# Moving the block boundary in a two-layer MoE decoder step to the front of the last expert round

## The chip, the cores and the metric

The kernel runs on one core of one Trainium2 chip. The metric is the device time of one execution in microseconds (us): lower is better. TensorE (PE) multiplies matrices into PSUM, VectorE (DVE) and ScalarE (ACT) work on rows, GpSimd (POOL) gathers and does odd jobs, SyncE (SP) does no arithmetic here and issues nearly all DMA transfers.

## The reference

One inference step of a two-layer trunk on 256 prompt tokens and 8 samples (264 columns, held transposed as 8 chunks of 128 features):

```python
for i in range(DEPTH):                      # DEPTH = 2
    mod = silu(c) @ ada_w[i] + ada_b[i]     # shifts, scales, gates: six groups of 1024
    h = modulate(x, norm_mix_g[i], sh1, sc1)
    m = retention_mixer(h, ...) if i % 2 == 0 else gla_mixer(h, ...)
    x = x + g1 * m
    h = modulate(x, norm_ffn_g[i], sh2, sc2)
    f = moe_ffn(h, ...)                     # 64 experts, 8 per token, and a shared one
    x = x + g2 * f
return rmsnorm(x, final_norm_g), new states
```

## The kernel before, in words

The program is a row of blocks: `retention`, `experts(k, 0)`, `gla`, `experts(k, 1)`, `final`. Each block (`with nc.Block()`) holds one instruction list per engine, and ends with a barrier of all five engines, SP among them. `experts` has two blocks: the main one, and a second one (line 3059) for the overflow, in which tokens are worked off that did not fit the slots of their expert. Every engine reads the number of pairs of overflow experts there (`pairs`) and branches over the body when it is 0, as it is with these inputs.

Weights come in 1 MB loads into a ring of 12 slots. `load_until` and `load_round` are SP's lists: for each load SP waits until the load 12 places earlier has been used (`ring_free`), then issues the transfer. TensorE adds to `ring_free` with its last matmul on a slot.

The main block works the 64 experts off in 16 rounds of four (`pe_round`, `round_` of VectorE and of ScalarE). Rounds 14 and 15 are light: each expert has 32 slots, and the whole round is one tile. A round on TensorE: gate products (line 2337), the spread of the round before (line 2395; VectorE adds each of 8 chunks to `acc`, `add_spread`, line 2803), up products, transposes, gathering for the next round, down products (line 2347). In round 15 (`LAST`) SP issues the down weights as eight half loads (line 2252), VectorE adds `acc` to `x` (`add_last`, 8 chunks of three instructions, lines 2806 to 2811), and `last_spread` (line 2380) spreads the round's own rows, which are added to `x` chunk by chunk. Behind these follows, in layer 0, the norm ahead of `gla` (`nxt`, squares at line 505, sums at 524, `Norm.vector`, `Norm.scalar` at 511 and 516) and `cond_products` (line 457); in layer 1 the transposes and sums of squares of the output (`x_rows`, `final_squares`).

Before, SP ends its list of the main block with six loads for the next stage (four of `ada_w`, two of `gla_w_in`), a wait for the remaining slots, and the branch at line 2259. Then come the main block's barrier, the overflow block with its five branches (TensorE's at line 3098) and its barrier, and the block of `gla`, in which SP first issues the two small loads `a1` and `a2` (lines 1316 and 1317), then the rest of the ring. TensorE begins with `project(0, ...)` (line 1361), which reads all 8 chunks of `hT` twice, and then multiplies by `a1` (line 1469).

Of the kernel before, what the change touches and what calls it, by code (L numbers as in the profile page):

```python
# [21 lines left out]
P = 128  # L22
D = 1024
# [106 lines left out]
def build(nc, inp, out):  # L130
    ctx = ExitStack()
    with ctx:
# [3 lines left out]
        def sb(name, cols, dt=F32, parts=P):  # L136
# [7 lines left out]
                    ["ret_state_stored"] + [f"ret_sample_state_stored{b}" for b in range(8)]  # L144
                    + ["gla_state_stored"] + [f"gla_sample_state_stored{b}" for b in range(4)]}
# [46 lines left out]
        experts(k, 0)  # L192
        gla(k)
        sums = experts(k, 1)
        final(k, sums)


# [293 lines left out]
class Norm:  # L491


    def __init__(self, k, layer, which, sq, tmp, root, bank, summed=False):
        self.k, self.layer, self.which = k, layer, which
        self.summed, self.sums_at = summed, k.ps[:, bank, 0:T]
        self.sq, self.tmp, self.root = sq, tmp, root
        self.s_ms, self.s_rt, self.s_prod, self.s_step = (k.sem(f"norm{layer}{which}_{n}") for n in (
            "meansq", "root", "scaled", "vector_step"))
        other = ("chunk", "samples") if summed else ("squared", "summed")  # L500
        self.s_h, self.s_samples = self.s_sq, self.s_sum = tuple(k.sem(f"norm{layer}{which}_{n}") for n in other)
# [5 lines left out]
    def scalar(self, act, next_table=None, turn=0):  # L507

        k, nc = self.k, self.k.nc
        act.wait_ge(self.s_ms, turn + 1)  # L510
# [3 lines left out]
        for c in range(DC):  # L514
            act.wait_ge(self.s_prod, DC * turn + c + 1)
            ins = nc.scalar.activation(k.h[:, c, 0:TP], k.h[:, c, 0:TP], ACT.Identity,
                                       bias=k.mod[:, self.layer, 3 * self.which, c, 0:1])
            if self.summed:
                ins.then_inc(self.s_h, 1)

    def sum(self, pe, c, turn=0):

        pe.wait_ge(self.s_sq, DC * turn + c + 1)
# [4 lines left out]
    def vector(self, v, turn=0):  # L528
# [3 lines left out]
        steps = [3 * turn]  # L532
# [6 lines left out]
        if not self.summed:  # L539
            v.wait_ge(self.s_sum, turn + 1)  # L540
        nc.vector.tensor_scalar(self.tmp, self.sums_at, 1.0 / D, EPS, ALU.mult, ALU.add).then_inc(self.s_ms, 1)
        v.wait_ge(self.s_rt, turn + 1)
# [5 lines left out]
        ins = nc.vector.tensor_tensor(hs, hs, k.mod[:, layer, 3 * which, :, 1:NCOND], ALU.add)  # L548
        if self.summed:
            ins.then_inc(self.s_samples, 1)  # L550
# [45 lines left out]
def retention(k):  # L596
# [60 lines left out]
    s_ldb = [k.stored[f"ret_sample_state_stored{b}"] for b in range(8)]  # L657
    c_out = k.stored["ret_state_stored"]
# [572 lines left out]
def gla(k):  # L1231
# [72 lines left out]
    s_stb = [k.stored[f"gla_sample_state_stored{i}"] for i in range(4)]  # L1304
    c_out = k.stored["gla_state_stored"]
# [7 lines left out]
    with nc.Block() as block:  # L1313
        @block.sync
        def _(sp):
            sp.dma_start(a1, inp["gla_w_a1"][0].rearrange("(c p) r -> p c r", p=P)).then_inc(s_w, 16)
# [7 lines left out]
        def _(pool):  # L1324
            clear_semaphores(pool, old)
            def free(i):
                pool.wait_ge(s_stb[i], 16)
# [3 lines left out]
            def store_prompt(h):  # L1331
                pool.wait_ge(c_s2, h + 1)
                if h:
                    pool.wait_ge(c_out, 16 * h)
# [19 lines left out]
            pool.wait_ge(c_out, 16 * GH)  # L1354

        @block.tensor
        def _(pe):
            def project(t, m, bank, chunks=range(DC)):
# [101 lines left out]
            for t in range(first_gate):  # L1460
# [3 lines left out]
                project(t, 0, 2 * (t % 2))  # L1464
# [7 lines left out]
                elif t == 1:  # L1472
                    pe.wait_ge(s_lowc, 1)
                    for h in range(GH):
                        if h >= 2:
                            pe.wait_ge(s_zc, h - 1)
                        nc.tensor.matmul(k.ps[:, 6 + h % 2, 0:T], a2[:, h * P:(h + 1) * P], low, start=True,
                                         stop=True).then_inc(s_z, 1)
                    cond_transpose(k, k.ps[:, 4], next_rows(k)).then_inc(s_crt, 1)
# [87 lines left out]
        def _(v):  # L1567
            link = lambda ins: k.dve.link(v, ins)
# [46 lines left out]
            def prompt_states(h):  # L1615
                v.wait_ge(s_st, h + 1)
                if h >= 2:
                    v.wait_ge(s_o, h - 1)
                    v.wait_ge(c_out, 16 * (h - 1))
# [147 lines left out]
        def _(act):  # L1767
            def outers(u):
# [156 lines left out]
def final_small(k, pe, small):  # L1925

    for c in range(DC):
        k.nc.tensor.matmul(k.ps[0:NS, 0, 0:1], small[:, c, :], k.ones[:, 0:1], start=(c == 0), stop=(c == DC - 1))


def final(k, sums):
# [5 lines left out]
    meansq, root, rstd = (k.scratch[:, (TT + 1) * D + 4 * i:(TT + 1) * D + 4 * i + TT] for i in range(3))  # L1937
    n_gain = k.stage["final_gain"]
    gain = slot(k, n_gain, D)[:, 0, :]

    with nc.Block() as block:  # L1941
        @block.scalar
        def _(act):
            act.wait_ge(s_ms, 1)
# [8 lines left out]
        def _(v):  # L1953
            nc.vector.scalar_tensor_tensor(meansq[:, 0:2], sums[:, 0:2], EPS, sums[:, 2:4], ALU.add, ALU.add)
# [14 lines left out]
        def _(pool):  # L1969
            wait_slot(k, pool, n_gain)  # L1970
            pool.wait_ge(s_scaled, 1)  # L1971
            nc.gpsimd.tensor_tensor(y[0:NS, 2, :], scaled[0:NS, :], gain[0:NS, :], ALU.mult).then_inc(s_small, 1)

        @block.sync
        def _(sp):
            for t in range(2):
# [9 lines left out]
def experts(k, layer):  # L1986
# [145 lines left out]
    number = extra[0:1, 0:1]  # L2132

# [91 lines left out]
    with nc.Block() as block:  # L2225
        @block.sync
        def _(sp):
# [26 lines left out]
            k.issued = n_end  # L2254
            load_until(k, sp, n_end + KEPT)
            for i in range(KEPT):
                sp.wait_ge(k.ring_free[(n_end + KEPT + i) % RING], (n_end + KEPT + i) // RING)
            sp.wait_ge(s_count, 2)
            with sp.If(sp.value_load(number, min_val=0, max_val=XPAIRS) > 0):
                load_extra(sp, X_LOADS, pair_experts(sp, 0))  # L2260

        @block.gpsimd
        def _(pool):
# [11 lines left out]
            for r in range(LAST + 1):  # L2275
# [5 lines left out]
                if r == 3:  # L2281
                    pool.wait_ge(s_hidtc, PAIRS * 2)
                    pool.wait_ge(s_hid, PAIRS * 2)
                    clear_semaphores(pool, routed)

# [81 lines left out]
        def last_spread(pe, behind):  # L2367
# [891 lines left out]
```

## Time and profile before

| | us |
|---|---|
| three runs | 1614.11, 1618.62, 1620.0 |
| their median | 1618.62 |
| the profiled execution's own time | 1614.77 |
| its span, first to last instruction | 1613.0 |
| TensorE busy | 1516.2 (94%) |
| VectorE, ScalarE, GpSimd busy | 709.3, 364.3, 94.0 |
| mean DMA rate | 360 GB/s, 580.21 MB |

TensorE has work in 94% of the span, and in the expert rounds the DMA engines are full as well. The mean hides the few places where TensorE stands: the change is made at two of these, once in each layer. Engine names with a q behind them are the engine's sequencer, which also executes waits, branches and the parts of a barrier (DRAIN, EVENT_SEMAPHORE).

### The profile page before, as it was taken

To read this page: it belongs to the slowest core of one execution; us is meant where nothing else is said; L and a number is where in the kernel's file an instruction comes from. 1 tells how busy PE (TensorE), PEld (TensorE's weight loads), DVE (VectorE), ACT (ScalarE), POOL (GpSimd) and SP (SyncE) were. 2 spreads that over 40 slices of the span, in tenths; PEclk is the share of its full clock that TensorE was granted. 3 is DMA by queue.
4 is the path that set the end of the run, shared out by engine and by line. 5 is a ranking of instruction groups with operands and counts; after the bars stand their busy time and mean duration, and the time that the engine had idled before them with its cause. 6 is when DMAs were issued, how large, how long until landed. Compare 5 with 4: busy or idle time off the path is not lost. (4 is left out here: it accounts for less than half of the span.)

```text
span 1613.0 us, 29632 instructions
## 1 busy us (share of the span) xinstructions
PE 1516.2 (94%) x11206; PEld 1009.5 (63%) x11206; DVE 709.3 (44%) x1980; ACT 364.3 (23%) x770; POOL 94.0 (6%) x119
## 2 busy tenths in 40 slices
PE   6999999998999999999997799999999999999986
PEld 4778765776665665565554487767566556565553
DVE  3205535215465355345454235443745534543453
ACT  3002443103111121112111244431111111211112
POOL 0000110001000000000000000001000000010000
PEclk9999999999999999999999899999999999999998
DMA  9997799339999999999999793988999999999896
GB/s 364 388 370 266 259 394 404 124 98 367 393 420 420 420 421 420 419 420 419 398 370 409 265 291 110 351 305 325 420 420 421 421 420 420 420 419 410 338 420 248
DMA packets 153578, 580.21 MB, mean 360 GB/s; under 512 B 17181, under 2 KB 62401, under 8 KB 105226
## 3 DMA queue, kind: packets, MB, share of 16 engines
q1 hardware_dynamic: 137642, 535.74, 83.8%
q0 software_dynamic: 15200, 40.92, 6.6%
q10 hardware_dynamic: 640, 2.26, 0.4%
q8 instruction: 61, 1.00, 0.3%
q14 instruction: 35, 0.29, 0.0%
HBM read 567.17 MB, written 26.90 MB: 368 GB/s over the span
## 5 line engine op out<-in xcount | busy, mean ns | idle before, releaser
L2431 PE MATMUL ps<-ring,scratch 128*64 128x256 f32 x3328 | 367.8, 380 | 10.0 <-DMA ring<-in_moe_w_up 8.8
L2431 PEld LDWEIGHTS ps<-ring,scratch 128*64 128x64 f32 x3328 | 245.0, 137 | 121.6 <-issue 14.3
L2497 PE MATMUL ps<-ring,scratch 128*64 128x512 f32 x896 | 200.5, 598 | 0.0
L698 PE MATMUL ps<-hT,ring 128*128 128x264 f32 x768 | 182.5, 392 | 1.3 <-ACT hT L380 1.3
L2836 DVE SCALAR_TENSOR_TENSOR scratch<-scratch,ps 128x256 f32<-128x256 f32 x62 | 29.8, 481 | 327.4 <-ACT scratch L2985 313.4
L2395 PE MATMUL ps<-scratch 128*128 128x264 bf16 x1392 | 169.6, 276 | 1.5 <-DVE scratch L2803 1.5
L698 PEld LDWEIGHTS ps<-hT,ring 128*128 128x128 f32 x768 | 147.6, 194 | 31.4 <-issue 2.8
L2395 PEld LDWEIGHTS ps<-scratch 128*128 128x128 bf16 x1392 | 121.8, 97 | 50.2 <-issue 14.3
L2803 DVE TENSOR_TENSOR scratch<-scratch,ps 128x264 f32<-128x264 f32 x240 | 102.6, 430 | 86.3 <-PE ps L2395 86.0
L2497 PEld LDWEIGHTS ps<-ring,scratch 128*64 128x64 f32 x896 | 58.1, 136 | 117.7 <-issue 86.2
L2985 ACT ACTIVATE scratch<-ps 128x256 f32<-128x256 f32 x62 | 23.8, 384 | 424.6 <-PE ps L2431 356.3
L2164 POOL DMA_INDIRECT scratch<-h_rows,scratch x60 | 59.8, 997 | 897.9 <-DVE scratch L2158 889.3
L3015 ACT CAST scratch<-ps 128x512 bf16<-128x512 f32 x116 | 68.0, 586 | 145.2 <-PE ps L2497 139.9
L1361 PE MATMUL ps<-hT,ring 128*128 128x264 f32 x384 | 91.9, 396 | 9.5 <-PEq L3059 9.5
L2897 DVE TENSOR_TENSOR scratch<-ps,scratch 128x512 f32<-128x512 f32 x116 | 79.7, 687 | 25.9 <-ACT scratch L3015 25.9
L1361 PEld LDWEIGHTS ps<-hT,ring 128*128 128x128 f32 x384 | 74.1, 196 | 23.4 <-issue 10.3
L2887 DVE TENSOR_TENSOR scratch<-scratch 128x512 bf16<-128x512 f32 x116 | 80.4, 693 | 4.0
L2311 PE MATMUL ps<-tab,scratch 128*128 128x128 f32 x480 | 65.1, 279 | 13.0 <-DVE scratch L2631 9.7
L2311 PEld LDWEIGHTS ps<-tab,scratch 128*128 128x128 f32 x480 | 51.8, 141 | 24.7 <-DVE scratch L2631 16.4
L955 DVE SCALAR_TENSOR_TENSOR ring<-ring,rstd 128x512 f32<-128x512 f32 x64 | 41.3, 687 | 49.7 <-ACT rstd L1108 36.7
L2631 DVE COPY scratch<-ps 128x512 f32<-128x512 f32 x60 | 41.5, 692 | 48.5 <-PE ps L2311 48.5
L859 PE MATMUL ps<-scratch,ring 128*128 128x264 f32 x256 | 57.7, 387 | 0.0
(402 smaller groups left out, 1458.3 us busy)
## 6 DMA issues: line engine op xcount, KB each, us to landing
ring<-in_moe_w_gate SPq DMA_DIRECT2D x128, 1024.0 KB, 20.1
ring<-in_moe_w_up SPq DMA_DIRECT2D x128, 1024.0 KB, 21.9
ring<-in_moe_w_down SPq DMA_DIRECT2D x120, 1024.0 KB, 18.0
ring<-in_ada_w SPq DMA_DIRECT2D x48, 1024.0 KB, 12.4
ring<-in_ret_w_in SPq DMA_DIRECT2D x24, 1024.0 KB, 16.7
ring<-in_state_ret SPq DMA_DIRECT2D x16, 1024.0 KB, 14.0
out_ret_sample<-ring POOLq DMA_DIRECT2D x16, 1024.0 KB, 9.2
ring<-in_gla_w_in SPq DMA_DIRECT2D x12, 1024.0 KB, 12.0
```

The source lines that it names most:

```text
L698: mm = nc.tensor.matmul(k.ps[:, bank, 0:T], w[:, c, m * P:(m + 1) * P], k.h[:, c, :], start=(c == 0), stop=(c == DC - 1))
L859: mm = nc.tensor.matmul(k.ps[:, out_bank(n), 0:T], w[:, c, m * P:(m + 1) * P], vo[:, 4 * h + c, :], start=(h == 0 and c == 0), stop=(h == ...
L1361: mm = nc.tensor.matmul(k.ps[:, bank, 0:T], w[:, c, m * P:(m + 1) * P], k.h[:, c, :], start=(c == 0), stop=(c == DC - 1))
L2164: pool.indirect_dma_start(xtok_of(p), None, h_rows[:, :], bass.IndirectOffsetOnAxis(ap=rows[:, p:p + 1], axis=0), bounds_check=ABSENT - 1, ...
L2311: mm = nc.tensor.transpose(k.ps[:, b, c * P:(c + 1) * P], xtok_of(p)[:, d0:d0 + P], ident)
L2395: mm = nc.tensor.matmul(k.ps[:, c % 2, 0:T], parts_of(p)[:, s, c * P:(c + 1) * P], slot_token[:, p, :], start=(p == 0 and s == 0), stop=(p ...
L2431: mm = nc.tensor.matmul(k.ps[lo:lo + CAP, 2 + p, j * DE:(j + 1) * DE], xg[:, p, c, lo:lo + CAP], slot(k, n, DE)[:, c, :], start=(c == 0), ...
L2497: mm = nc.tensor.matmul(k.ps[lo:lo + CAP, 6 + half, :], hid_t[:, p, m, lo:lo + CAP], slot(k, n, D)[:, m, half * 512:(half + 1) * 512], sta ...
L2803: nc.vector.tensor_tensor(acc[:, c, :], acc[:, c, :], k.ps[:, c % 2, 0:T], ALU.add).then_inc(s_add, 1)
L2887: nc.vector.tensor_tensor(parts_of(p)[:, 2, cols], rest[:, half], parts_of(p)[:, 1, cols], ALU.subtract).then_inc(s_part, 1)
L2897: nc.vector.tensor_tensor(rest[:, half], k.ps[:, 6 + half, :], parts_of(p)[:, 0, cols], ALU.subtract).then_inc(s_rest, 1)
L3015: nc.scalar.copy(parts_of(p)[:, 0, cols], k.ps[:, 6 + half, :]).then_inc(s_rhi, 1)
```

## The change

The main block of `experts` now ends after round 14. All that follows is returned as an object `tail` with one function per engine, which `gla` (or `final`) calls at the top of its own block: the last round, the overflow path, the norm behind it (in layer 1 the output's sums). The overflow block is gone. Each engine reads the number of pairs at the end of the main block (`read_pairs`, a wait, a register load and a check) and takes one branch at the top of the next block: with pairs, round 15 and the overflow; without (`Else`), round 15 and the following sums. SP's loads of round 15 stay in the main block. Its loads of the next stage come behind the barrier: twelve without a wait for an overflow, then a wait for the norm's sums (`behind.norm.s_sum`), then `a1` and `a2`. `gla`'s first projection waits for `hT` chunk by chunk. In round 14 VectorE adds `acc` to `x` ahead of `hidden`, and in round 15 adds the spread of round 14 straight to `x` (three instructions a chunk in place of one). ScalarE runs a dummy square root in both layers behind the branch. Clearing of semaphores moves to the end of `gla`'s GpSimd list, and one set of store semaphores serves both mixers.

```diff
 experts: SP, end of main block
-            k.issued = n_end
-            load_until(k, sp, n_end + KEPT)
-            for i in range(KEPT):
-                sp.wait_ge(k.ring_free[(n_end + KEPT + i) % RING], (n_end + KEPT + i) // RING)
-            sp.wait_ge(s_count, 2)
-            with sp.If(sp.value_load(number, min_val=0, max_val=XPAIRS) > 0):
-                load_extra(sp, X_LOADS, pair_experts(sp, 0))
+            read_pairs(sp, "sp")
...
 experts: TensorE, end of main block
-            for r in range(HEAVY - 2, LAST + 1):
+            for r in range(HEAVY - 2, LAST):
                 pe_round(pe, r)
-            last_spread(pe, x_rows if layer else nxt.sum)
...
+            read_pairs(pe, "pe")
...
+        def vector_round(v, r, late=0, beside=None):
...
+            if last:
+                for c in range(DC):
+                    v.wait_ge(s_scat, DC * (r - 1) + c + 1)
+                    add_last(v, c, k.ps[:, c % 2, 0:T], DC + c).then_inc(s_add, 1)
+            elif light(r):
+                add_spread(v, r - 1)
+                v.wait_ge(s_add, DC * (r + 1))
+                for c in range(DC):
+                    ins = add_last(v, c, acc[:, c, :], c)
+                k.dve.link(v, ins)
...
+    def tail_sync(sp):
+
+        k.issued = n_end
+        load_until(k, sp, n_end + KEPT)
+        pairs = extra_pairs["sp"]
+        with sp.If(pairs > 0):
...
+        load_until(k, sp, n_end + RING)
...
+    def tail_tensor(pe):
...
+        with pe.If(pairs > 0):
+            pe_round(pe, LAST)
+            last_spread(pe, None)
...
+        with pe.Else():
+            pe_round(pe, LAST)
+            last_spread(pe, follow)
+            for c in range(DC - 2, DC):
+                follow(pe, c)
...
+        nc.scalar.activation(silu[0:1, 0, 0:1], ident[0:1, 0:1], ACT.Sqrt)
...
 gla
         @block.sync
         def _(sp):
+            behind.sync(sp)
+            sp.wait_ge(behind.norm.s_sum, 1)
             sp.dma_start(a1, inp["gla_w_a1"][0].rearrange("(c p) r -> p c r", p=P)).then_inc(s_w, 16)
...
+                    if first:
+                        pe.wait_ge(behind.norm.s_h, c + 1)
```

## Rows read from the trace of the kernel before

**Rows 1.** Windows: stretch, its length, busy us by engine, PEclk, DMA share, GB/s.

```profile
840.00:850.00 10.00, 10.00 (x112) 5.72 (x109) 6.95 (x17) 1.56 (x3) 0.99 (x1) 1.00 1.02 423
...
912.00:914.00 2.00, 2.00 (x6) 1.58 (x5) 0.00 (x0) 0.00 (x0) 0.00 (x0) 0.50 0.67 178
...
916.00:918.00 2.00, 2.00 (x11) 1.71 (x10) 0.00 (x0) 0.00 (x0) 0.00 (x0) 1.00 1.10 348
```

**Rows 2.** Timeline, TensorE in round 15 of layer 0: start, us, what, [idle before].

```profile
866.58 5.89 PE L2337 MATMUL ps<-ring,scratch 128*32 128x256 f32 x64 [5.33 <-DMA ring<-in_moe_w_gate]
872.40 0.85 PE L2395 MATMUL ps<-scratch 128*128 128x264 bf16 x6
...
876.53 3.66 PE L2337 MATMUL ps<-ring,scratch 128*32 128x256 f32 x64
```

**Rows 3.** Timeline of SP's issues around the same round, and its last piece alone.

```profile
861.73 15.41 SPq L2252 DMA_DIRECT2D ring<-in_moe_w_down  x8
877.18 5.12 SPq L300 DMA_DIRECT2D ring<-in_ada_w  x4
882.34 10.51 SPq L300 DMA_DIRECT2D ring<-in_gla_w_in  x2
...
876.08 1.05 SPq L2252 DMA_DIRECT2D ring<-in_moe_w_down  x1
```

**Rows 4.** Sources of two barriers, lines 2225 and 1313: duration in ns, first and last start.

```profile
L2225 SPq DRAIN  x2: 7/7/7, 893.9 to 1598.4; - x2
...
L1313 PEldq DRAIN  x1: 737/737/737, 1067.8 to 1067.8; - x1
L1313 SPq DRAIN  x1: 116/116/116, 1069.2 to 1069.2; - x1
L1313 SPq EVENT_SEMAPHORE  x1: 17/17/17, 1069.5 to 1069.5; - x1
```

**Rows 5.** Source of TensorE's overflow branch, min/median/max ns, layer 0 and layer 1.

```profile
L3098 PEldq COMPARE_BRANCH  x2: 334/2028/3722, 905.4 to 1604.6; - x2
```

**Rows 6.** Timeline, VectorE: adding two chunks of a spread, then chunks added to x.

```profile
873.05 0.77 DVE L2803 TENSOR_TENSOR scratch<-scratch,ps 128x264 f32<-128x264 f32 x2 [9.04 <-PE ps L2395]
...
885.43 0.17 DVE L2806 TENSOR_TENSOR scratch<-ps,mod 128x8 f32<-128x8 f32 x1 [0.24 <-PE ps L2380]
...
885.98 0.16 DVE L2806 TENSOR_TENSOR scratch<-ps,mod 128x8 f32<-128x8 f32 x1
```

**Rows 7.** Timeline from the norm of layer 0 into the next mixer.

```profile
900.52 3.30 ACT L516 ACTIVATE hT<-hT,mod 128x256 f32<-128x256 f32 x8 [3.04 <-DVE hT L552]
...
909.55 10.30 PE L1361 MATMUL ps<-hT,ring 128*128 128x264 f32 x32 [9.46 <-PEq L3059]
...
919.78 3.73 PE L1469 MATMUL ps<-hT,scratch 128*16 128x264 f32 x16
...
923.45 7.39 PE L1361 MATMUL ps<-hT,ring 128*128 128x264 f32 x32
```

**Rows 8.** DMA issues of 855 to 925: KB each, median us from issue to landing.

```profile
ring<-in_ada_w SPq DMA_DIRECT2D x4, 1024.0 KB, 14.4
scratch<-in_gla_w_a SPq DMA_DIRECT2D x1, 64.0 KB, 2.6
```

**Rows 9.** Timeline of layer 1: TensorE in round 15, SP's last two pieces.

```profile
1574.39 5.27 PE L2337 MATMUL ps<-ring,scratch 128*32 128x256 f32 x64 [5.96 <-DMA ring<-in_moe_w_gate]
...
1584.33 3.66 PE L2337 MATMUL ps<-ring,scratch 128*32 128x256 f32 x64 [0.60 <-DMA ring<-in_moe_w_up]
...
1582.38 1.71 SPq L2252 DMA_DIRECT2D ring<-in_moe_w_down  x2
```

**Rows 10.** Timeline of the end: ScalarE's last sum, then the final block.

```profile
1598.99 0.20 ACT L3039 ACTIVATE scratch<-tab 1x1 f32<-1x1 f32 x1
...
1603.29 0.20 ACT L1920 ACTIVATION_READ_ACCUMULATOR scratch<-ps 128x1 f32 x1
1605.35 1.28 ACT L1945 ACT_TABLE_LOAD   x1 [1.86 <-PEq L3059]
...
1606.64 0.20 ACT L1945 ACTIVATE scratch<-scratch 128x3 f32<-128x3 f32 x1
```

More of the change, by code:

```diff
@@ L191, in build @@
         retention(k)
[L192 to L195, printed above, removed]
+        behind = experts(k, 0)
+        gla(k, behind)
+        behind = experts(k, 1)
+        final(k, behind)
 def retire_semaphores(k):
@@ L497, in __init__, with scalar @@
         self.sq, self.tmp, self.root = sq, tmp, root
[L498 to L501, printed above, removed]
+        self.s_ms, self.s_rt, self.s_prod, self.s_step, self.s_h, self.s_samples = (
+            k.sem(f"norm{layer}{which}_{n}") for n in ("meansq", "root", "scaled", "vector_step", "chunk", "samples"))
+        if not summed:
+            self.s_sq, self.s_sum = (k.sem(f"norm{layer}{which}_{n}") for n in ("squared", "summed"))
     def square(self, act, c):
         return self.k.nc.scalar.activation(self.sq[:, c, :], self.k.x[:, c, :], ACT.Square).then_inc(self.s_sq, 1)
-    def scalar(self, act, next_table=None, turn=0):
+    def scalar(self, act, next_table=None):
         k, nc = self.k, self.k.nc
-        act.wait_ge(self.s_ms, turn + 1)
+        act.wait_ge(self.s_ms, 1)
         nc.scalar.activation(self.root, self.tmp, ACT.Sqrt).then_inc(self.s_rt, 1)
@@ L1228, with gla @@
 GLA_OUT_BANK = [0, 1, 2, 4, 5, 6, 3, 7]
-def gla(k):
+def gla(k, behind):
     nc, inp, out = k.nc, k.inp, k.out
@@ L1463, in _ @@
                     pe.wait_ge(s_qk, 2 * (t - 1))
-                project(t, 0, 2 * (t % 2))
+                if t == 0:
+                    pe.wait_ge(behind.norm.s_samples, 1)
+                project(t, 0, 2 * (t % 2), first=t == 0)
                 project(t, 1, 2 * (t % 2) + 1).then_inc(k.ring_free[loads[t] % RING], 1)
@@ L1767, in _ @@
         def _(act):
+            behind.scalar(act)
             def outers(u):
@@ L1927, in final_small, with final @@
     for c in range(DC):
-        k.nc.tensor.matmul(k.ps[0:NS, 0, 0:1], small[:, c, :], k.ones[:, 0:1], start=(c == 0), stop=(c == DC - 1))
-def final(k, sums):
+        mm = k.nc.tensor.matmul(k.ps[0:NS, 0, 0:1], small[:, c, :], k.ones[:, 0:1], start=(c == 0), stop=(c == DC - 1))
+    return mm
+def final(k, behind):
     nc, out = k.nc, k.out
@@ L1943, in _ @@
         def _(act):
+            behind.scalar(act)
             act.wait_ge(s_ms, 1)
@@ L2365, in slots_first, with last_spread @@
             mm.then_inc(s_ht, 1)
-        def last_spread(pe, behind):
+        def last_spread(pe, follow):
             d = done_tiles(LAST, 0)
@@ L2381, in last_spread @@
                                      start=True, stop=True).then_inc(s_scat, 1)
-                    if half:
-                        behind(pe, c - 2)
+                    if half and follow:
+                        follow(pe, c - 2)
         def spread(pe, r, late=0, n=PAIRS):
```

758 lines of the change are left out of this document (380 added, 378 removed).

## The prediction

> **What bounds the kernel now.** I read the windows first. In the expert rounds TensorE is busy for the whole of a window and the DMA engines are full too, at 423 GB/s [rows 1]; a delay handed to TensorE there is not won back later, since neither has slack. Then I went to the two places which the change touches and read the timeline of every engine there, because what counts at a barrier is who arrives last. Three things are to be seen.
>
> First, TensorE stands before round 15 in both layers: the gate products start at 866.58 after 5.33 us of waiting for weights, in layer 1 at 1574.39 [rows 2, 9]. Second, SP is later still: its eight half loads of the down weights take 15.41 us to issue, the last ends at 876.08 + 1.05 = 877.13, and only at 877.18 does it issue the loads whose slots TensorE gave back around 872.4 [rows 2, 3]. SP is held by the transfer queue being full, not by a semaphore. Third, the old boundary comes after all this: ScalarE's last `hT` chunk is done at 900.52 + 3.30 = 903.82, TensorE starts the projections at 909.55, 9.46 us after its last matmul [rows 7].
>
> **The barrier, which moves.** It includes SP: SP has a DRAIN in the main block's barrier at 893.9, 1.05 us behind its last issue (882.34 + 10.51 = 892.85), and in that time it had read `pairs` and branched [rows 3, 4]. In the barrier that closes the `gla` block SP is the last: TensorE has drained at 1067.8 + 0.74 = 1068.5, SP at 1069.2 + 0.12 = 1069.3, and the release is at 1069.5, 0.2 us later [rows 4]. SP's drain does not wait for transfers in flight, only for its own list.
>
> The change leaves SP's eight half loads ahead of the barrier and puts TensorE's round 15 behind it. So round 15, which now waits for the gate weights until 866.58, will wait for SP to have *issued* the last down weights. SP arrives at 877.13 + 1.05 = 878.2, the release is at 878.4. Queued behind it: round 15 on TensorE, VectorE and ScalarE, the norm, the ring's next loads.
>
> **The branch.** TensorE's branch over the overflow body took 3.72 us in layer 0 and 0.33 us in layer 1, the same instruction with the same outcome [rows 5]. The new branch jumps over a body that holds all of round 15 as well, so its target is further away. I take 3.72 us in both layers; 0.33 us is the lower bound. For the upper bound I take two such stalls, 7.44 us, since the new branch runs while the queues are full, and the old ones did not.
>
> The Trainium skill ("Runtime: NRT & Kernel Launch", Instruction fetch mechanics) says that a taken branch with a target outside the fetched window stalls for a fetch, which agrees with the slow row, and that TensorE's instruction memory holds 2048 instructions, more than this body; by that figure the target could be there after the long wait at the barrier, and the sum would be that of the short branch.
>
> **Layer 0, in order.**
> - Round 15 starts at 878.4 + 3.7 + 0.1 = 882.2 in place of 866.58: +15.6 (12.2 with the short branch).
> - Gate products took 5.89 us after a pause of 5.33, and 3.66 for the same 64 at full clock [rows 2]. After the 9.46 us pause the projections still ran at 0.50 until 914 and at 1.00 from 916: 10.30 us against 7.39 [rows 1, 7], so about 2.9 us extra. The new pause is some 20 us. Between 5.89 and twice 3.66 = 7.3 I take 6.5, near 3.66 + 2.9: +0.6.
> - The spread of round 14 now ends in three VectorE instructions a chunk, at a pitch of 0.55 us (885.43 to 885.98), in place of 0.385 (0.77 for two) [rows 6]. TensorE alternates two banks, so each pair of chunks waits once for a VectorE step that is 0.17 longer, four times: about +0.5 with a hand-over.
> - `acc` added to `x` in round 14 instead of round 15: 8 x 0.55 = 4.4 us of VectorE. Removed from round 15 it gains nothing: after it VectorE still waited 0.24 us for TensorE [rows 6]. Added to round 14 it stands ahead of `hidden` and delays that round by some 1.3 us, which is covered: TensorE ended round 14 at 866.58 - 5.33 = 861.25 [rows 2], 17 us before SP arrives. Without that cover it would cost the 1.3 us.
> - Dummy square root: 0.20 us [rows 10], on the path in layer 0. +0.2.
> - So the norm is +16.9. Its `hT` chunks come from 900.94 + 16.9 = 917.8 to 920.7. With the chunk-wise wait and no barrier, the first eight-chunk pass takes 3.7 us (half of 7.39) from 917.9 and ends at 921.6, the second at 925.3. The clock should be full, the pause being under 1 us. Before, this point was 919.78 [rows 7]: +5.5. The change thus saves 11.4 us here, 5.7 of barrier and branch, 2.8 of overlap, 2.9 of clock, and gives 16.9 for it.
> - `a1` now stands behind twelve ring loads in SP's queue. The first four can start when the gates are done, 882.2 + 6.5 = 888.7; at 2.7 us each (386 GB/s) and eight at 3.0 us (1.05 MB at 348 GB/s [rows 1]) the stream ends at 923.5, and `a1` needs 2.6 us from issue to landing on an empty queue [rows 8], so 924 to 926. TensorE wants it at 925.3. I put +0.5, with 0 and 3 as ends.
> Sum of layer 0: +6.0.
>
> The Trainium skill ("DMA: Bandwidth & Descriptors", Queues, rings and completion order) says that completion is not in order per issuing engine, by which `a1` might land ahead of the last ring loads; the term would then be 0.
>
> Semaphore clearing moves behind GpSimd's last wait of `gla`, where the block's end is set by SP and TensorE [rows 4]; nothing, and what it would cost without that cover are some register-sized instructions on GpSimd. Store semaphores shared: nothing. The rounds and `gla` between are bound by TensorE, so the shift is carried whole.
>
> **Layer 1.** SP's last piece ends at 1582.38 + 1.71 = 1584.09 [rows 9]; + 1.05 + 0.2 + 3.7 + 0.1 = 1589.2 against 1574.39: +14.8. Gates 6.5 for 5.27: +1.2. Spread +0.5, less the 0.60 that the up products waited for weights [rows 9]. Together +15.9 to ScalarE's last sum. Gained behind it: from 1603.49 to the square root at 1606.64 lie two barriers and a table load of 1.28 us [rows 10]; in one list, behind a square root already run, what remains is three small VectorE instructions, about 0.55 us: -2.6. Sum: +13.3.
>
> **Total.** 6.0 + 13.3 = +19.3. On the profiled execution: 1614.8 + 19.3 = 1634.1. The median of the runs is 3.9 above it, which would give 1637.9; the lowest run is 0.7 below it. I give 1636.
>
> **Rivals.**
> - *Short branch.* Both branches cost 0.33: -3.4 in layer 1; in layer 0 about -2.5, as `a1` then lands after TensorE wants it. 1628 on the profile, up to 1632. For it: layer 1's row.
> - *Longer stalls.* Two fetches behind full queues, or `a1` 3 us late: +8 to +11, 1642 to 1648.
> - *SP does not hold the barrier.* If it has issued its last load by the time the gates land (866.6), round 15 starts when it did. Then TensorE wants `a1` at about 908.5, but the twelve loads cannot end before some 921 (the round's own four up and eight half down loads end at 866.6 + 8 x 2.48 = 886.4 at 423 GB/s, then 34.8 for the twelve), so layer 0 is still +2 to +3 and layer 1 -2.6 + 0.5: no change, 1615. Against it: the rows of SP.
> - *Faster.* As before, and `a1` passes the ring loads. Then layer 0 gains 11.4 less 1: the mechanism is the whole old boundary leaving the path, at two places. Layer 0 gains as long as round 15 starts less than 11.4 - 1.3 = 10.1 us late, before 876.7, so with 4.0 for release and branch SP must arrive before 872.7. Full price, with SP there before the gates land: 1614.8 - 10.4 - 2.1 = 1602. Against it: SP arrives at 878.2 in this trace, and issues the same list at the same rate afterwards.
>
> **How the numbers follow.** Forecast 0.60, short branch 0.15, longer stalls 0.12, SP early 0.07, faster 0.06. The measurement can tell about 0.5%, 8 us, from no change. Slower by more: 0.60 + 0.15 + 0.12 = 0.87; within: 0.07; faster: 0.06. Range 1624 to 1648: it takes in the first three cases.
>
> **What would show it.** In the new trace: the main block's barrier with SP draining last, near 878 and 1585; gates of round 15 starting near 882 and 1589 with the barrier as releaser, in place of a DMA; TensorE's branch row, of 0.3 or 3.7 us; the DMA engines empty for a few us before the `ada_w` loads; `project` starting about 1 us behind the norm's first chunk; ScalarE's last square root without a table load. If SP drains before 867, the forecast is wrong at its root; if the gates start below 880 it is the branch that I have mis-sized.

## The result and the profile after

| | before | after |
|---|---|---|
| median of four runs, us | 1617.43 | 1641.47 |
| lowest to highest, us | 1614.11 to 1620.0 | 1640.37 to 1643.62 |
| the profiled execution's own time | 1614.77 | 1642.50 |
| its span | 1613.0 | 1640.7 |

The changed kernel is slower: the ratio is 1.0151, with an interval of 1.0128 to 1.0175. That is +24.0 us between the medians and +27.7 between the two spans. The difference between these is the choice of executions: the profiled one before lies 2.7 below its median, the one after 1.0 above it. What follows compares spans.

The page of after shows where the time is not. TensorE is busy for as long as before (1516.2 then), and nearly the same bytes are moved (580.21 MB then):

```profile
PE 1517.1 (92%) x11206; PEld 1006.4 (61%) x11206; DVE 712.9 (43%) x2012; ACT 363.5 (22%) x770; POOL 94.1 (6%) x119
...
DMA packets 153580, 580.23 MB, mean 354 GB/s; under 512 B 17181, under 2 KB 62401, under 8 KB 105226
```

So the 27.7 us are time in which TensorE stands, waits or runs at its lower clock. TensorE's timeline around round 15 of layer 0, answering to [rows 2], shows most of one half of it:

```profile
858.57 0.50 PE L2434 MATMUL ps<-tab,scratch 128*128 128x128 f32 x2 [1.98 <-DVE scratch L2768]
...
885.59 5.46 PE L2359 MATMUL ps<-ring,scratch 128*32 128x256 f32 x64 [21.94 <-issue]
890.98 0.85 PE L2418 MATMUL ps<-scratch 128*128 128x264 bf16 x6
...
895.83 3.66 PE L2359 MATMUL ps<-ring,scratch 128*32 128x256 f32 x64
```

The gate products of round 15 start at 885.59, after a pause of 21.94 us; before, at 866.58 after 5.33 [rows 2]. The releaser is no DMA any more. Who held TensorE is in two other views: SP's timeline, and the source rows of the barrier, of the branch behind it and of VectorE's branch (duration in ns, start in layer 0 to start in layer 1).

```profile
864.12 13.82 SPq L2279 DMA_DIRECT2D ring<-in_moe_w_down  x8
...
1581.74 14.32 SPq L2279 DMA_DIRECT2D ring<-in_moe_w_down  x8
```

```profile
L2252 PEldq DRAIN  x2: 2032/2124/2215, 861.8 to 1579.5; - x2
L2252 ACTq DRAIN  x2: 14/16/18, 864.6 to 1582.5; - x2
L2252 DVEq DRAIN  x2: 95/96/97, 866.3 to 1584.2; - x2
L2252 SPq DRAIN  x2: 7/7/7, 878.6 to 1596.7; - x2
...
L2252 PEldq EVENT_SEMAPHORE  x2: 51/51/51, 878.8 to 1596.9; - x2
...
L3106 PEldq COMPARE_BRANCH  x2: 6212/6224/6237, 878.9 to 1597.0; - x2
...
L3179 DVEq COMPARE_BRANCH  x2: 63/63/63, 878.9 to 1597.0; - x2
```

Read down the starts of the DRAINs. VectorE is ready at 866.3 and SP at 878.6, so four engines stand for 12 us for one that is still issuing transfers. Its eight half loads end at 864.12 + 13.82 = 877.94, and the release follows 0.2 us behind its drain. The last four of the eight wait for no semaphore (`ring_free` stands ahead of the first four only), and their issues take 1.0 to 4.5 us each, where the quickest of the eight take 0.5: SP is held in issuing itself, while the DMA engines are full. Then TensorE's branch takes 6.2 us, in both layers. The late round also empties the memory system: SP's next loads wait for slots that round 15 gives back, and the first of them is issued at 891.06. The window ahead of it (the last number is the rate in GB/s; the kernel before has 408 in the same window):

```profile
885.00:890.00 5.00, 4.41 (x49) 2.44 (x52) 0.00 (x0) 0.00 (x0) 0.00 (x0) 0.57 0.26 97
```

Further on in layer 0, at the seam to the next mixer (timeline, answering to [rows 7]):

```profile
919.72 3.30 ACT L515 ACTIVATE hT<-hT,mod 128x256 f32<-128x256 f32 x8 [3.05 <-DVE hT L547]
...
920.37 7.36 PE L1364 MATMUL ps<-hT,ring 128*128 128x264 f32 x32 [1.17 <-ACT hT L515]
...
920.40 2.92 SPq L1314 DMA_DIRECT2D scratch<-in_gla_w_a  x1
923.36 2.92 SPq L1315 DMA_DIRECT2D scratch<-in_gla_w_a  x1
...
930.26 5.39 PE L1474 MATMUL ps<-hT,scratch 128*16 128x264 f32 x16 [2.54 <-DMA scratch<-in_gla_w_a]
...
935.59 7.39 PE L1364 MATMUL ps<-hT,ring 128*128 128x264 f32 x32
```

The first projection starts beside the norm, 0.65 us behind its first chunk, where before 9 us lay between [rows 7]: the gain that the change has here is real. But the 16 products with `a1` start 2.54 us after TensorE could have begun them, and take 5.39 us at a lower clock for 3.73. By 935.59 the shift is +12.1.

Which transfer they waited for has to be read from the code as well. `a1` (line 1314) and `a2` (line 1315) raise one semaphore, and TensorE waits ahead of the `a1` products until both have landed (`pe.wait_ge(s_w, 32)`, with 16 for each load), though `a2` is multiplied only one projection later. The view of the DMA issues:

```profile
scratch<-in_gla_w_a SPq DMA_DIRECT2D x1, 64.0 KB, 7.9
scratch<-in_gla_w_a SPq DMA_DIRECT2D x1, 32.0 KB, 6.9
```

`a2` has landed at 923.36 + 6.9 = 930.26, and this is when the products start. `a1` is put at 920.40 + 7.9 = 928.3, 0.6 us behind the end of the projection (920.37 + 7.36 = 927.7); as both raise one semaphore, the split between them is the profile's estimate. So the last to come is `a2`.

Layer 1, round 15 and the end (timeline, answering to [rows 9, 10]):

```profile
1603.59 6.55 PE L2359 MATMUL ps<-ring,scratch 128*32 128x256 f32 x64 [22.02 <-issue]
...
1633.77 0.20 ACT L1929 ACTIVATION_READ_ACCUMULATOR scratch<-ps 128x1 f32 x1
...
1634.39 0.20 ACT L1957 ACTIVATE scratch<-scratch 128x3 f32<-128x3 f32 x1 [0.42 <-DVE scratch L1971]
```

The gates start 29.2 us later than before, of which 11.9 are brought along (the barrier at the end of `gla` is released at 1081.4, before at 1069.5). From ScalarE's last sum to the square root are 0.62 us and no table load, in place of 3.35 with one [rows 10].

### The profile page after: what moved, and what is told of

The parts are those of the page before. It is cut to its first block and busy times, and to the rows that moved or that the text cites. A ratio compares the mean times of both kernels' runs of the same rounds, so it can differ in the third digit from the quotient of the medians.

```text
span 1640.7 us, 29626 instructions
## 1 busy us (share of the span) xinstructions
PE 1517.1 (92%) x11206; PEld 1006.4 (61%) x11206; DVE 712.9 (43%) x2012; ACT 363.5 (22%) x770; POOL 94.1 (6%) x119
## 5 line engine op out<-in xcount | busy, mean ns | idle before, releaser
L2735 DVE TENSOR_TENSOR scratch<-scratch,ps 128x264 f32<-128x264 f32 x224 | 96.4, 431 | 66.3 <-PE ps L2418 66.0
L2359 PE MATMUL ps<-ring,scratch 128*32 128x256 f32 x512 | 34.0, 424 | 44.0 <-issue 44.0
## 6 DMA issues: line engine op xcount, KB each, us to landing
ring<-in_gla_w_in SPq DMA_DIRECT2D x12, 1024.0 KB, 11.5
```

Of the source, the lines that this page charges most:

```text
L2359: mm = nc.tensor.matmul(k.ps[lo:lo + 32, bank, j * DE:(j + 1) * DE], xg_of(p)[:, c, lo:lo + 32], slot(k, n, DE)[:, c, :], start=(c == 0), ...
L2735: nc.vector.tensor_tensor(acc[:, c, :], acc[:, c, :], k.ps[:, c % 2, 0:T], ALU.add).then_inc(s_add, 1)
```

## The experiments

Three causes are in the trace: SP, the branch, and the wait for `a1` and `a2`. The rivals are that they cover each other (whoever takes away one finds the next), or that the round is held by something else behind the barrier: the empty transfer queues, or the three instructions a chunk. Each cause is taken away alone, then all three together, and one part of the change is put into the kernel before by itself. Each kernel's ratio is to the kernel before on its own chip (thirteen runs with a median of 1615.34 for the first four, 29 with 1615.22 for the others). The changed kernel's own ratio rests on only four runs before, so what a kernel takes away from it is given twice, by the medians and by the ratios (times 1616):

| kernel | median | ratio | less than after: by medians | by ratios |
|---|---|---|---|---|
| half loads behind the barrier | 1624.75 | 1.0057 | 16.7 | 15.2 |
| shortened body | 1638.85 | 1.0143 | 2.6 | 1.3 |
| empty body | 1629.47 | 1.0088 | 12.0 | 10.2 |
| early `a1` | 1638.70 | 1.0134 | 2.8 | 2.7 |
| loads, `a1` and empty body | 1608.01 | 0.9960 | 33.5 | 30.9 |
| exchanged bodies | 1635.07 | 1.0128 | 6.4 | 3.7 |
| loads, `a1` and exchanged bodies | 1612.06 | 0.9982 | 29.4 | 27.3 |

**SP's list: the eight half loads go behind the barrier.**

```diff
 experts: SP, main block
-            expert_of = [expert_at(sp, LAST * EPI + e) for e in range(EPI)]
-            for half in range(2):
...
-                    sp.dma_start(slot(k, n, D)[:, :, cols], expert_weight("moe_w_down", expert_of[e])[:, :, cols])\
-                        .then_inc(s_first_half if half == 0 else k.ring_full[n % RING], 16)
             read_pairs(sp, "sp")
...
     def tail_sync(sp):
+        expert_of = [expert_at(sp, LAST * EPI + e) for e in range(EPI)]
+        for half in range(2):
...
```

> The changed kernel with one edit: SP issues round 15's eight down-weight loads behind the barrier, as the first thing in the next block, in place of ahead of it. Theory (the barrier waits for SP's issuing): VectorE now drains last, near 866.3, the release is near 866.5, and with the same 6.2 us branch the gate products of round 15 start near 873.3 in layer 0 (885.6 in the changed kernel) and near 1591 less what layer 0 gains in layer 1 (1603.6). Layer 1 gains about 12. Layer 0 gains only about 4 of its 12, because the small load a1 still stands behind twelve ring loads, whose stream cannot begin before the round's own weights are in. Sum about -15 to -16 against the changed kernel: 1.005 to 1.007 of the kernel before, near 1626. Rival (the barrier is held by something else, such as the transfers in flight): the start stays at 885, ratio 1.015.

Measured: 1624.75 (ten runs), ratio 1.0057 (1.0038 to 1.0075), as expected. Barrier, branch and round of that kernel:

```profile
L2252 SPq DRAIN  x2: 7/7/7, 857.4 to 1568.6; - x2
...
L2252 DVEq DRAIN  x2: 97/99/101, 866.3 to 1575.9; - x2
L3108 PEldq COMPARE_BRANCH  x2: 6189/6200/6212, 866.7 to 1576.3; - x2
...
873.24 6.29 PE L2350 MATMUL ps<-ring,scratch 128*32 128x256 f32 x64 [9.59 <-issue]
...
922.49 5.48 PE L1474 MATMUL ps<-hT,scratch 128*16 128x264 f32 x16 [6.29 <-DMA scratch<-in_gla_w_a]
```

Now SP drains first and VectorE last, at 866.3 as in after, and the gates start 12.35 us earlier, which is the stretch from 866.3 to 878.6. That SP held the barrier is thereby shown, not read off alone. The branch is as long with SP's list out of its way, so its 6.2 us don't hang on the long wait ahead of it (between TensorE's last product and the branch lie 3 us here and 15 there). And the wait for `a1` and `a2` has grown from 2.54 to 6.29 us: TensorE came 11.5 us earlier, the issue of `a2` only 7.8. This is a cause covered by another.

**The branch: the body that is jumped over is shortened.** First, of TensorE's body with pairs, the last round is left out and the overflow kept:

```diff
         with pe.If(pairs > 0):
-            pe_round(pe, LAST)
-            last_spread(pe, None)
...
```

> The changed kernel with one edit: on TensorE the body that is branched over holds the overflow alone, as in the kernel before, without round 15 (left out is thus round 15 in the case of an overflow, which these inputs don't have). Theory (the stall of 6.2 us comes from the length of the jump): it falls to 0.3 to 3.7 us, as in the kernel before, in each layer; -5 to -12 in sum, 1630 to 1636. Rival (it comes from full transfer queues, which the branch of the kernel before did not meet): it stays at 6.2 us in both layers and the time at 1641.

Measured: 1638.85 (four runs), ratio 1.0143 (1.0111 to 1.0175): a miss. The branch is as short as was expected, and the time hardly moved. The rows say why:

```profile
L3106 PEldq COMPARE_BRANCH  x2: 342/354/367, 878.7 to 1595.2; - x2
...
879.43 1.03 PE L2359 MATMUL ps<-ring,scratch 128*32 128x256 f32 x2 [16.06 <-PEq L2252]
885.33 5.16 PE L2359 MATMUL ps<-ring,scratch 128*32 128x256 f32 x62 [4.87 <-issue]
```

The round begins at 879.43, executes two products, and then stands for 4.87 us, with "issue" as its releaser, which means nothing that the profile shows. In layer 1 the same happens with 2.10 us, after 29 products. So the stall is not bound to the branch instruction. My reading is that it is the time until instructions of the new place are there: in layer 0 the first 2 products were at hand, in layer 1 the first 29. Why the same body differs so between the layers, these runs don't say; in both the stall ends 6.4 to 6.6 us behind the start of the branch, much as in the changed kernel (6.2). Whoever reads the branch row alone takes this for a gain of 6 us.

The profile bears the reading out. In its view of the DMA queues one transfer on a queue that it calls "instruction" lies within the 6.2 us of the branch in after (window 878.9 to 885.1 in layer 0):

```profile
q8 instruction: 1, 0.02, 1.1%
```

Narrowed down, it starts at 882.55 and takes 1.05 us (layer 1: 1600.73 and 1.15). In each stall of these traces there is one such transfer, of 16 KB, and TensorE goes on 1.3 to 1.6 us behind its end: both layers of this kernel, of after, of the one with the half loads moved and of the one with early `a1`, layer 0 of the exchanged bodies below, and the slow branch of the kernel before. There it starts 1.0 us behind the branch, in after 3.7, which is about the difference between 3.7 and 6.2 us. Such transfers also occur where nothing stands, so it is the constant distance that speaks, not their presence.

Then the whole body is left out, one wait remains:

```diff
         with pe.If(pairs > 0):
-            pe_round(pe, LAST)
...
-            for c in range(DC):
-                follow(pe, c)
```

> The changed kernel with one edit: on TensorE the body that is branched over holds one wait and nothing else (left out is the overflow's arithmetic, not needed with these inputs). Theory (the stall is a fetch of instructions for a far target): 0.1 to 0.35 us in both layers, gates of round 15 start at 879.5 in place of 885.6; about -6 in each layer, 1629 to 1630, ratio 1.007 to 1.008. Rival (any taken branch behind a barrier costs this): 6.2 us stays.

Measured: 1629.47 (four runs), ratio 1.0088 (1.0057 to 1.0119), as expected.

```profile
L3106 PEldq COMPARE_BRANCH  x2: 213/220/226, 877.9 to 1590.2; - x2
...
878.58 5.07 PE L2359 MATMUL ps<-ring,scratch 128*32 128x256 f32 x64 [15.93 <-PEq L2252]
...
923.34 6.65 PE L1474 MATMUL ps<-hT,scratch 128*16 128x264 f32 x16 [3.02 <-DMA scratch<-in_gla_w_a]
```

All 64 gate products run through from 878.58, with no second stall. The jump thus costs 6.0 us a layer (6.22 less 0.22; a further 1.0 us of the earlier start in layer 0 is SP, which was through at 877.6 in this execution). It is the distance that costs: the comparison, the outcome and the barrier ahead of it are the same.

**`a1`: a copy of it loaded ahead of the ring loads, to a place that is free then.**

```diff
-    a1 = on_flat[:, 0:DC * RANK].rearrange("p (c r) -> p c r", c=DC)
+    a1 = k.rstd[:, 2 * T:2 * T + DC * RANK].rearrange("p (c r) -> p c r", c=DC)
...
         def _(sp):
+            sp.dma_start(a1, inp["gla_w_a1"][0].rearrange("(c p) r -> p c r", p=P)).then_inc(s_w1, 16)
             behind.sync(sp)
...
-                    pe.wait_ge(s_w, 32)
+                    pe.wait_ge(s_w1, 16)
...
+                    pe.wait_ge(s_w, 16)
```

The edit does two things: `a1` comes early, and its products no longer wait for `a2`, which is waited for one projection later (the last line, with the products of `a2`).

> The changed kernel with one edit: the small load a1 goes to a place that is free already and is issued at the start of the next block, ahead of the ring loads, with a semaphore of its own; a2 stays behind. Theory (a1 behind twelve ring loads costs 2.5 us of waiting and 1.7 us of slower products after it): -4.2 us, all in layer 0, 1637, ratio 1.012 to 1.013; the products with a1 take 3.7 us again in place of 5.4 and start without a DMA in front. Rival (TensorE then waits for something else, such as the next ring load): no gain.

Measured: 1638.7 (four runs), ratio 1.0134 (1.0102 to 1.0166), as expected. Its interval overlaps with that of after, so the runs alone don't separate the two; the trace does:

```profile
881.16 0.41 SPq L1313 DMA_DIRECT2D rstd<-in_gla_w_a  x1
...
923.28 7.36 PE L1365 MATMUL ps<-hT,ring 128*128 128x264 f32 x32 [1.17 <-ACT hT L515]
930.57 3.73 PE L1475 MATMUL ps<-hT,rstd 128*16 128x264 f32 x16
934.24 7.39 PE L1365 MATMUL ps<-hT,ring 128*128 128x264 f32 x32
```

From the first projection to the second are 934.24 - 923.28 = 10.96 us, in after 935.59 - 920.37 = 15.22. So the wait for the two costs 4.3 us, 2.5 of standing and 1.7 of clock. How much of it the split of the semaphore alone would have saved was not run. This execution came 2.9 us later to the first projection (round 14 was late already, ahead of the place that the edit touches), which hides it in the time.

**All three together** (half loads behind the barrier, early `a1`, no body to jump over):

> The changed kernel with three edits together: down loads behind the barrier, a1 ahead of the ring loads (behind the down loads), and on TensorE a body to branch over that holds one wait (left out is the overflow's arithmetic on TensorE, not needed with these inputs). Theory (three costs, and nothing else, stand between the change and its gain): round 15 starts when its gate weights are in, near 868, as in the kernel before; layer 0 is 9 to 10 us ahead of the kernel before at the products with a1, layer 1 gains another 1 to 2 at the end. Sum -9 to -12 against the kernel before, ratio 0.993 to 0.995. Rival (the moved work has a cost of its own that the three hide): ratio 0.998 or above.

Measured: 1608.01 (ten runs), ratio 0.996 (0.9948 to 0.9973). This is faster than the kernel before, by 7.2 us between the medians, but less than was expected (9 to 12, 0.993 to 0.995; only the interval reaches into that). Alone, the three took away 31.5 by the medians and 28.1 by the ratios; together they take away 33.5 and 30.9. Within the noise, some 3 us for each ratio, they add up. But a fourth cost has come out from behind them.

```profile
868.01 5.28 PE L2352 MATMUL ps<-ring,scratch 128*32 128x256 f32 x64 [4.45 <-DMA ring<-in_moe_w_gate]
...
903.36 7.36 PE L1365 MATMUL ps<-hT,ring 128*128 128x264 f32 x32 [1.16 <-ACT hT L515]
910.65 3.73 PE L1475 MATMUL ps<-hT,rstd 128*16 128x264 f32 x16
...
924.45 3.15 PE L1484 MATMUL ps<-scratch 16*128 16x264 f32 x8 [2.75 <-DMA scratch<-in_gla_w_a]
```

The gates wait for their weights again, as before the change, and `a1` is multiplied 9.1 us earlier than before it (910.65 to 919.78 [rows 7]). This is what the moved boundary is worth when nothing holds it: the 11.4 us that the prediction's sum has for the barrier, the overlap and the clock, less the 1.4 by which the gates start later and the 0.7 of the longer spread.

Of the 9.1 us most is lost again at the next small load. `a2` was left behind the ring loads, is issued at 914.78 and takes 9.5 us to land, and its products at 924.45 wait 2.75 us for it. Behind the pause the granted clock (the last column but two) is at half:

```profile
926.00:928.00 2.00, 2.00 (x6) 1.07 (x5) 0.00 (x0) 0.93 (x3) 0.00 (x0) 0.50 1.09 346
```

From these products to the same later point of the mixer (975.00, before 978.03) it takes 50.55 us, before 47.26: 3.3 us more. So 2.75 + 3.3 = 6.0 of the 9.1 us are gone; 3.0 are left at that point and 3.3 at the end of `gla`. In layer 1 the gates start 3.9 us earlier than before, the end brings another 2.7, and 6.6 is what the spans differ by (1606.4 to 1613.0). None of the other kernels waits there, since in each the `a2` products come later or an earlier wait has covered `a2`. `a2` loaded early as well was not run; by these rows, as an estimate, it would bring up to 6 us more.

**The same, with the overflow kept: TensorE's two bodies change places.** The last round without overflow stands directly behind the branch, the one with overflow behind it, so that the far jump comes after the round.

```diff
-        with pe.If(pairs > 0):
+        with pe.If(pairs < 1):
+            pe_round(pe, LAST)
+            last_spread(pe, follow)
...
+        with pe.Else():
             pe_round(pe, LAST)
             last_spread(pe, None)
...
```

Alone on the changed kernel:

> The changed kernel with the exchange of TensorE's two bodies alone. Theory: round 15 starts 6 us earlier in both layers, at 879.5 and accordingly; layer 1 keeps the 6, layer 0 gives the stall back between the sums and the projection, but then no longer waits for a1, so it keeps 3 to 4.5. Sum -9 to -11 against the changed kernel, 1631, ratio 1.009 to 1.010. Rival (the jump behind the sums costs nothing): as with the empty body, 1629 or less, ratio 1.008.

Measured: 1635.07 (four runs), ratio 1.0128 (1.0113 to 1.0143): a miss, less of a gain than was expected.

```profile
L3106 PEldq COMPARE_BRANCH  x4: 83/2460/6609, 879.1 to 1622.8; - x4
...
879.61 6.16 PE L2359 MATMUL ps<-ring,scratch 128*32 128x256 f32 x64 [15.62 <-PEq L2252]
...
916.26 6.59 PE L456 MATMUL ps<-ring,condT 128*32 128x256 f32 x64 [5.95 <-issue]
...
933.77 7.39 PE L1364 MATMUL ps<-hT,ring 128*128 128x264 f32 x32
```

The 6.0 us are won at the gates (879.61 for 885.59), and in layer 0 lost again behind the norm's sums: TensorE stands for 5.95 us at the jump to the common code (6609 ns in the branch row is this jump), and the 64 products behind the pause take 6.59 us for 3.66. The windows of this stretch show the granted clock (the last column but two) at half, 1.2 GHz, from the pause on:

```profile
914.00:916.00 2.00, 0.00 (x0) 0.00 (x0) 2.00 (x6) 1.58 (x4) 0.00 (x0) 0.50 1.07 353
...
918.00:920.00 2.00, 2.00 (x24) 0.96 (x20) 0.63 (x2) 0.00 (x0) 0.00 (x0) 0.50 1.14 356
```

The norm of the other engines goes on meanwhile and hides a part; the second projection starts 1.8 us earlier than in after, and no more. In layer 1 this jump comes at 1622.8, behind TensorE's last product, and is over after 4.84 us, while the last stores are still going out, so that nothing waits for it directly. Of the 8.4 us by which the span is shorter, 6.6 come from layer 1. It could have been 8.4 there: the last square root comes 10.2 us earlier (1624.20 for 1634.39), but from it to the end it takes 8.1 us for 6.3, as SP is released later behind its last stores; why, these runs don't say. (By the ratios the gain is only 3.7; the profiled execution is this kernel's fastest, and the ratio of after rests on few runs. How much of the miss is that stays open.)

All three, with the bodies exchanged:

> The same, but with the overflow kept: on TensorE the two bodies are exchanged, so that the one without overflow is fallen into and the jump over the overflow's body stands behind it; in layer 1 nothing follows the jump, in layer 0 the products with the condition and the next mixer do. Theory: layer 1 pays nothing for the jump; layer 0 pays 5 to 6 us between the norm's sums and the first projection, where only about 1 us was free. Sum -3 to -6 against the kernel before, ratio 0.996 to 0.998. Rival (a jump at the end of a straight run is fetched ahead): as the run without a jump, 0.993 to 0.995.

Measured: 1612.06 (twelve runs), ratio 0.9982 (0.9972 to 0.9993), on the side of faster, at the weak edge of what was expected, and by less than the 0.5% that the prediction wanted to call it a change.

```profile
869.50 5.35 PE L2352 MATMUL ps<-ring,scratch 128*32 128x256 f32 x64 [3.82 <-DMA ring<-in_moe_w_gate]
...
906.39 5.85 PE L456 MATMUL ps<-ring,condT 128*32 128x256 f32 x64 [5.94 <-issue]
```

Of the versions that still work off an overflow, this is the fastest. The one without a jump is 4 us faster. The row of `L456` has the jump, 5.94 us and a lower clock behind it; it is more than 4, but TensorE comes late enough for `a2` here and doesn't pay the 6.0 us that the other pays there.

**`acc` into `x` in round 14, alone on the kernel before:**

```diff
+                if last:
+                    for c in range(DC):
+                        v.wait_ge(s_scat, DC * (r - 1) + c + 1)
+                        add_last(c, k.ps[:, c % 2, 0:T], DC + c).then_inc(s_add, 1)
+                elif light(r):
                     add_spread(r - 1)
...
+                        ins = add_last(c, acc[:, c, :], c)
```

> The kernel before with one part of the change alone: the accumulator is added to x in round 14, and round 15 adds the spread of round 14 straight to x. Theory (the part costs little and gains nothing by itself): round 14 on TensorE ends 1.3 us later, covered by the wait for the gate weights at 866.6; the spread in round 15 takes 4.9 us in place of 4.1, in layer 1 hidden behind the up weights. Sum 0 to +1.5 us, ratio 1.000 to 1.001. Rival (the 4.4 us of VectorE taken out of round 15 had been on the path): -4 to -8 us, ratio 0.995 to 0.998.

Measured: 1615.04 (ten runs), ratio 0.9998 (0.9986 to 1.0009). This part moves nothing that can be measured, by itself too: its 1.3 us in round 14 fall into the wait for round 15's gate weights.

## Why the prediction was right, and where its sizes were off

The direction was right, and so was the mechanism at its root: SP's drain came last in the barrier, forecast at 878.2, measured at 878.6; in layer 1, with the shift of 11.9 brought along, 1597.0 was forecast and 1596.7 measured. Undoing that alone took away 15.2 us by the ratios, of 24.4.

The time was forecast as 1636 and measured as 1641.5; on the profiled execution, 1634.1 against 1642.5. So 8.4 us are missing from the sum. Two terms hold them, and a third is small.

- *The branch.* The term was 3.7 us in each layer, the slow one of the two rows of the kernel before [rows 5], and it measured 6.2: 2.5 twice. It lies between my value and the upper bound of two stalls, 7.4. The choice went wrong at a step that I had written down, that the target is further away, and then not priced: I took the row of a short jump for a long one. The empty body shows 0.2, the shortened one 0.35 with 4.9 us one place later. The rule of the Trainium skill ("Runtime: NRT & Kernel Launch", Instruction fetch mechanics) that a taken branch out of the fetched window stalls for a fetch agrees with the long rows and with the instruction transfer inside each stall; it leaves open why the same branch took 0.33 us in layer 1 of the kernel before. That the target might be there after the long wait, which I had worked out from that page's size of the instruction memory, did not come true, neither after 15 us of waiting nor after 3.
- *`a1`.* The term was 0.5 us with 3 as its upper end; it measured 4.2, outside my bounds. What failed first is a wait that the sum left out. I had priced the landing of `a1` alone, and the products wait for `a1` and `a2` on one semaphore. `a2` is issued 2.96 us behind `a1`, as the issue of `a1` itself holds SP for 2.92 us, and needs 6.9 us to land. By the profile's split `a1` was late by 0.6 us, near my 0.5, and the other 1.9 us of standing are `a2`. That the 0.5 fits so well is in part luck, since both sides of it lay later than I had them, TensorE at 927.7 for 925.3 and `a1` at 928.3 for 924 to 926. I had used the 2.6 us of an empty queue [rows 8], and the landings took 7.9 and 6.9.
  Both stood behind megabytes of ring loads that were issued but not through, and I had let the stream end first and then added the latency of an idle queue. The second omission is the clock: even a wait of 2.5 us cost 1.7 more in the products behind it (5.39 for 3.73), which the bound of 3 did not hold. Windows of after, in the pause and behind it:

```profile
928.00:930.00 2.00, 0.00 (x0) 0.00 (x0) 0.00 (x0) 0.42 (x2) 0.00 (x0) 1.00 1.09 331
930.00:932.00 2.00, 1.74 (x5) 0.58 (x5) 0.00 (x0) 0.00 (x0) 0.00 (x0) 0.56 1.08 349
```

  By the rule of the Trainium skill ("DMA: Bandwidth & Descriptors", Queues, rings and completion order) that completion isn't in order the term would have been 0. The trace agrees with the rule in a small way: the ring load issued just ahead at 917.43 took 12.1 us and landed at 929.5, 1.2 us behind where the profile puts `a1`. But that was not enough to make the wait vanish; what brought it to 0 was the issue ahead of the ring loads, with a semaphore of its own.
- *The start of the round and the gates in layer 0.* SP 0.4 later and the first product 0.5 instead of 0.1 behind the branch; against that, the gate products took 5.4 (from 885.59 to 890.98) for 6.5. With the 0.2 of the longer spread this comes to -0.1. In layer 1, 6.5 was forecast and 6.5 measured.

The rest held. The spread: 4.85 us for 4.13, so +0.7 for a forecast of +0.5. The dummy square root and the chunk-wise start of the first projection: shift of +19.2 at the norm's last step and of +7.95 at the end of the first projection, so 11.3 us saved there for a forecast of 11.4. The end of layer 1: -2.7 for -2.6. `acc` in round 14: nothing, and the run by itself says so too; its 1.3 us are in the trace (the transposes of round 14 waited 1.98 us for VectorE, with 0.68 before) and covered. And layer 0's sum, 6.0 + 2.4 (the branch's 2.5 less that 0.1) + 3.7 = 12.1, and layer 1's, 13.3 + 2.5 = 15.8, meet the 11.9 and 15.8 of the spans.

Of the rivals, the short branch and SP's being early are out by the rows. "Longer stalls", 1642 to 1648, came nearest in its mechanism: a longer fetch and a late small load. (Full queues as its reason were not tested by themselves.) The measured time lies 0.5 below its lower end, and I had given it 0.12. The forecast's own 0.60 was too much for a sum whose two soft terms could only be seen at shorter jumps and in an empty queue. The rival that ends on the faster side was not this kernel's case, but its mechanism, the old boundary leaving the path, is what the kernel with all three taken away shows. The rival's full price was 1602, 12.8 below the profiled execution; the runs give 7.2 between the medians. The trace has where the rest went: 6.0 us to the wait for `a2` and the clock behind it. Small parts are gates that start 1.4 us later than before and a wait of 0.35 us for the up weights in layer 0, where before there was none.

Open is how far a jump may go before it costs. Three lengths were run, and what the shortest of them left standing was one wait.

## What to carry to other kernels

Before moving a barrier, write down when each engine arrives at the new place, the one that only issues transfers too: a full transfer queue holds it as surely as a semaphore, and here that was over half of the loss. Price a jump by its distance, and look for its stall at the first instructions behind it, not in the branch row alone; a rare path is best laid so that the common path never jumps over it where somebody waits. A small transfer that is needed early has to be issued ahead of the large ones: behind them it took 7 to 10 us to land where 2.6 sufficed, and the wait cost clock on top. Before pricing a transfer, read the wait in the code: if it counts two transfers, the later one sets it. And after taking a cost away, look in the new trace for the next wait, which the old costs had covered.

## What the runs showed of the hardware

- A taken far jump on TensorE took 6.2 us in both layers, with 15 us of waiting ahead of it or 3. At another place (the exchanged bodies) TensorE stood 5.95 us for it, and at the very end of the kernel its row has 4.84 us. With a shorter one the branch took 0.35 us and the stall came 2 products later (4.87 us) or 29 products later (2.10 us).
- In each of these stalls, except the one at the very end, which no product follows, TensorE went on 1.3 to 1.6 us behind the end of a transfer of 16 KB on the queue named "instruction".
- VectorE stands as well, in layer 0 alone, and its branch row doesn't show it: 63 ns at 878.9, and its first operation of the new block comes at 884.59, 5.7 us behind the branch; in layer 1 at 1597.51, 0.5 us behind it. The other kernels with the moved boundary have 5.4 to 5.8 us in layer 0. That this too is a fetch is likely and not shown. TensorE's own jump hid it, and where that was gone the gate products did: with the empty body VectorE's first operation came at 883.64, as these ended (878.58 + 5.07). This is a timeline row of after:

```profile
884.59 0.20 DVE L2178 SCALAR_TENSOR_TENSOR scratch<-ps,tab 128x36 f32<-128x36 f32 x1 [18.30 <-issue]
```

- A transfer of 64 KB took 7.9 us from issue to landing behind ring loads, and 2.6 without them [rows 8]; the issue instruction itself held SP for 2.92 us. In the kernel with early `a1` it held SP for 0.41 us only, and yet the transfer took 9.5 us to land, behind the half loads of the down weights: a short issue doesn't tell of a quick landing.
- A wait of 2.54 us ahead of the `a1` products was followed by 5.39 us for 3.73 at a granted clock of 0.56 and 0.58; one of 2.75 us ahead of the `a2` products (all three taken away) by a clock of 0.50 from 926 to 932 and 3.3 us of extra time.
- Behind the pauses of 6 us ahead of `L456` its 64 products took 6.59 and 5.85 us for 3.66, at a granted clock of 0.50 in the first case: such a pause costs 2.2 to 2.9 us more than itself.
